# Two hybrid diffusion layers on one core: moving TensorE's streamed operands to other byte offsets

## What is computed

```python
for l in range(2):
    m  = split(silu(c) @ w_ada[l] + b_ada[l], 9)          # shift, scale, gate per part
    h  = h + 0.5 * m[2] * swiglu(modulate(rmsnorm(h)), w_in, w_out)      # 1024 -> 2*2816 -> 1024
    z  = modulate(rmsnorm(h)); p = z @ w_in_mix                          # 1024 -> 2048
    y  = concat(rg_lru_scans(p) * gelu(p), spatial_gate(p))
    h  = h + m[5] * (y @ w_out_mix)                                      # 1024 -> 1024
    h  = h + 0.5 * m[8] * swiglu(modulate(rmsnorm(h)), w_in, w_out)
return rmsnorm(h)
```

## Time and profile before

| | |
|---|---|
| two runs | 1577.13 and 1584.26 us, median 1580.7 us |
| span of the profiled execution | 1575.5 us |
| what lies around the span in the two runs | 1.6 and 8.8 us (5.2 at the median) |
| TensorE busy | 1561.2 us (99%), 9052 matmuls |
| weight loads busy | 1338.1 us (85%) |
| VectorE, ScalarE, GpSimd busy | 1001.6, 631.0, 82.5 us |
| from memory | 247.62 MB, 158 GB/s over the span |

### The profile page before, as it was taken

One profiled execution on the slowest core, in us unless ns is written; L12 is line 12 of the kernel. 1 busy time (PEld: TensorE's weight loads), 2 busy tenths in 40 slices (PEclk: granted clock), 3 DMA queues, 4 the chain that ended last, 5 costly groups with the idle time before them and its releaser, 6 DMA issues.

```text
span 1575.5 us, 22302 instructions
## 1 busy us (share of the span) xinstructions
PE 1561.2 (99%) x9052; PEld 1338.1 (85%) x9052; DVE 1001.6 (64%) x1243; ACT 631.0 (40%) x856; POOL 82.5 (5%) x100
## 2 busy tenths in 40 slices
PE   8999999999999999999999999999999999999998
PEld 6888888888988888888888898888888897999998
DVE  5776773783967577777364267777445358975554
ACT  4433322332784343323222243333232249764553
POOL 0000000011100200000000100000000111000001
PEclk9999999999999999999999999999999999999999
DMA  9565553653322355565353336556354323456563
GB/s 365 201 197 179 186 162 119 208 192 94 115 75 79 94 166 193 176 201 173 107 196 99 107 121 201 193 183 195 100 173 148 107 91 108 147 188 197 190 203 117
DMA packets 71786, 249.95 MB, mean 159 GB/s; under 512 B 11664, under 2 KB 11920, under 8 KB 70672
## 3 DMA queue, kind: packets, MB, share of 16 engines
q1 hardware_dynamic: 71696, 248.70, 48.1%
HBM read 247.62 MB, written 1.05 MB: 158 GB/s over the span
## 4 chain that ended last, share of the span: by engine, by line
PE 96%; DVE 2%; ACT 1%; issue 0%; POOL 0%; POOLq 0%; DVEq 0%; ACTq 0%
PE bank L437 85%; PE bank L574 2%; PE bank L580 2%; PE bank L576 2%; PE bank L452 1%; PE bank L475 1%; PE bank L747 1%; PE bank L720 1%; PE bank L718 1%; PE bank L719 1%; PE bank L749 0%; PE bank L468 0%; DVE w_lo L1174 0%; PE bank L529 0%; PE bank L460 0%
## 5 line engine op out<-in xcount | busy, mean ns | idle before, releaser
L877 ACT ACTIVATE w_hi<-raw 128x1024 fp32r<-128x1024 f32 x317 | 335.9, 1060 | 807.0 <-PE bank L437 792.8
L1174 DVE TENSOR_TENSOR w_lo<-raw,w_hi 128x1024 fp32r<-128x1024 f32 x317 | 387.7, 1225 | 371.9 <-ACT w_hi L877 371.6
L437 PE MATMUL bank<-z_hi,w_hi 128*128 128x512 f32 (+1 forms) x1480 | 535.9, 362 | 2.4 <-DVE w_lo L1174 1.9
L437 PE MATMUL bank<-z_lo,w_hi 128*128 128x512 f32 (+1 forms) x1480 | 532.1, 360 | 0.0
L437 PE MATMUL bank<-z_hi,w_lo 128*128 128x512 f32 (+1 forms) x1480 | 531.9, 359 | 0.0
L437 PEld LDWEIGHTS bank<-z_hi,w_hi 128*128 128x128 f32 x1480 | 278.0, 188 | 49.7 <-DVE w_lo L1174 3.2
L437 PEld LDWEIGHTS bank<-z_hi,w_lo 128*128 128x128 f32 x1480 | 278.0, 188 | 42.6
L437 PEld LDWEIGHTS bank<-z_lo,w_hi 128*128 128x128 f32 x1480 | 278.1, 188 | 42.6 <-issue 1.0
L437 PE MATMUL bank<-h_hi,w_hi 128*128 128x512 f32 (+1 forms) x770 | 266.5, 346 | 0.0
L437 PE MATMUL bank<-h_lo,w_hi 128*128 128x512 f32 (+1 forms) x770 | 265.7, 345 | 0.0
L437 PE MATMUL bank<-h_hi,w_lo 128*128 128x512 f32 (+1 forms) x770 | 265.6, 345 | 0.0
(11 more groups left out here) (185 smaller groups left out, 1234.3 us busy)
## 6 DMA issues: line engine op xcount, KB each, us to landing
raw<-weights SPq DMA_DIRECT2D x320, 512.0 KB, 4.1
ada_raw<-ada_w SPq DMA_DIRECT2D x128, 512.0 KB, 4.2
ada_head<-head_w SPq DMA_DIRECT2D x8, 1024.0 KB, 18.5
res<-x_t SPq DMA_DIRECT2D x4, 512.0 KB, 4.8
ada_raw<-gate_w SPq DMA_DIRECT2D x4, 256.0 KB, 5.3
ws<-sgu_w SPq DMA_DIRECT2D x2, 256.0 KB, 4.0
bs<-sgu_b SPq DMA_DIRECT2D x2, 256.0 KB, 4.2
out<-final SPq DMA_DIRECT2D x2, 256.0 KB, 3.0
```

What stands on the lines that cost most here:

```text
L437: m = pe.matmul(bank[:, to], w, x[:, k, at], start=start and i == 0, stop=stop and i == 2, skip_group_check=True)
L877: act.activation(w_hi[:, r, :], raw[:, r, :], ACT.Copy).then_inc(hi_ready, 1)
L1174: dve.tensor_tensor(w_lo[:, r, :], raw[:, r, :], w_hi[:, r, :].bitcast(F32), ALU.subtract).then_inc(lo_ready, 1)
```

## The change

Three unused tensors are added to the layout: 32 bytes ahead of `down_acc` and `z`, 96 bytes ahead of `raw`, and 96 bytes ahead of everything that shares the last space. Nothing else is changed: each engine has the same instructions in the same order, on other addresses. Lines of the kernel after are 1 to 3 higher (L437 is L440).

```diff
         res = sb("res", [P, KD, T])
 
+        sb("z_shift", [P, 8])
         with ExitStack() as down_scope:
             down_acc = [sb(f"down_acc{i}", [P, 2, D], F32, down_scope) for i in range(2)]
         with ExitStack() as end_scope:
             final = sb("final", [P, KD, SEQ], F32, end_scope)
         z_hi = sb("z_hi", [P, KD, T], F32R)
         z_lo = sb("z_lo", [P, KD, T], F32R)
+        sb("raw_shift", [P, 24])
         raw = sb("raw", [P, RING, SLOT])
...
         base_gain = sb("base_gain", [P, KD])
 
+        sb("h_shift", [P, 24])
         with ExitStack() as head_scope:
```

## The result

The changed kernel takes **1620.6 us** (median of two runs, 1620.42 and 1620.78) against 1580.7 before: 1.0251 of the time, with a 95% interval of 1.0209 to 1.0292. It is slower, and lies just above the range.

A forecast was written before the change was run, and what follows sets the result against it. TensorE's own pace was taken to bound the kernel (busy 1561.2 of 1575.5 us). The mean of three estimates (-41, -34, -15), -30 us, gave a span of 1545.5, plus 5.2 for the runs' median: 1551 us, range 1528 to 1620.

The forecast's parts named there:

- What a new offset is worth: TensorE matmuls: gain from distances of 32 or 96 bytes, drawn from the paces at 0 and 64; mean -30 us.
- three ways of going on: TensorE matmuls: left-over as a step (-41), a slope over offsets (-34), or by distance, 32 and 96 halfway (-15).
- The bounds of the pace: TensorE: below, streaming alone, 213.3 ns wide, 1502 us; above, 0.24 us per wide matmul, 1655 us.
- The slower rival: L437, TensorE: distances 32 or 96 never settle, wide 22 us more, ALONE 10.6 more; 1613 us (1600 to 1650), chance 0.29.
- disturbed pace: Where the gate matmuls disturb the even 226.7 ns, nine wide ones take 231.1 ns each; the slower rival's ground.
- The rival of no change: TensorE: left-over has another cause, or wide settles at 32 columns at any offset; 1581 us (1570 to 1590), chance 0.22.
- The 6198 matmuls: TensorE matmuls counted as moving against their weights from offset 0: 4938 wide and 1260 narrow.
- The rest of the change costs nothing: VectorE, ScalarE and DMA at offsets 32 and 96 cost nothing; `ada_head` landing 0 to 2 us, taken as 0.
- z and h would differ: Sign in the timeline's wide matmuls: if they differ, the slope is right, h near 217 ns, z near 223.
- The rule of the Trainium skill: TensorE has two independent SBUF read ports, weight loads take no bandwidth; an offset is worth nothing, the time stays.

The follow-up runs named there:

- The table: Short kernels without the computation: fp32r matmuls at 35 stream-to-weights distances, 512 and 256 columns wide; at distance 0, 226.7 and 120.0 ns between starts.
- the short kernels: Kernels of matmul stretches only, without the computation, varying distance, load width, start moment or type; wide fp32r at distance 0 with full loads: 226.7 ns.
- the kernel changed by 64: Against the kernel before, z and h both lie 64 bytes further from their weights, by three unused tensors: 1609.61 us, 1.0186 of before.

## Why the prediction was wrong

**The step that failed is "What a new offset is worth".** It took the 6.7 ns that 256-column matmuls have less at "64" for what 512-column ones would gain, and drew lines from there to 32 and 96. The table shows that a distance that is good for one width isn't so for the other, and that wide ones can only lose: 4938 of them sat on their best distance. All three ways of going on (-41, -34, -15 us) rested on it. Its second fault is the unit: within 128 bytes, the 192 of the `ALONE` columns looked like 64, and z's 160 like 32. The good distances of the two widths, 0 for 512 columns and 192 for 256, were taken as points on one line.

**The bounds of the pace.** 213.3 ns was a poor lower end; no wide fp32r stretch here came under 226.7. The upper one, 240 ns, held: the worst measured is 237.9.

**The slower rival** (0.29) was the right case: a distance of 32 or 96 off the weights doesn't reach the settled 226.7, and `ALONE` is taken off its good place. Its terms against what was measured: 22 us for wide ones, from 231.1 ns, where z takes 234.3 to 234.9, h and y 233.3 to 233.8, so some 24 + 10 + 0.7 = 35; 10.6 us for `ALONE`, where z lost 6.4 (984 x 6.5) and h 1.8, since 32 keeps half of the gain: 8. In sum 43 and not 33. The rows that I took for a disturbed pace were a passage of seven matmuls, of 228 to 236 ns, after which TensorE settled on 226.7 again. The timeline of the kernel before, just behind it:

```profile
421.75 0.39 PE L718 MATMUL bank<-w_hi,z_hi 128*128 128x512 f32 x1
...
422.43 0.39 PE L718 MATMUL bank<-w_hi,z_hi 128*128 128x512 f32 x1
```

Three matmuls in 0.68 us are 226.7 ns each. A wrong distance isn't a disturbance that goes on, but a pattern of its own, and a longer one. The rival also says "never settle", which is wrong in the words: it does settle, in the short kernels within some ten matmuls, and for good.

**The rival of no change** is refuted in both its grounds. The loops don't make 113.3 (in the kernel changed by 64 they run at 120), and only at distance 0 do wide matmuls with full loads settle on 32 columns over their stream, not at any distance. What spoke for it, `y_alone` at 117.7, was the second pace of distance 192.

**What held.** TensorE's pace goes through to the end one for one (42.6 of 43.1 us). The 6198 matmuls and the `ALONE` ones were the right ones to count. "The rest of the change costs nothing": means and landings are those of before, and `ada_head` at offset 96 lands in 18.4 us; z's first wide matmul behind those on the last piece of `ada_head` starts at 40.4 us instead of 39.7, within the 0 to 2 us I allowed. That z and h would differ, and that `ALONE` would show whether "64" was good of its own, were the right things to look at.

**The rule of the Trainium skill** that I set against the change, two independent read ports in "TensorE: Matmul & The Clock Gate", "Step-by-step: what each phase is for", makes an offset worth nothing. For bf16 at 512 columns this case agrees: 215.8 ns at eight distances. The same page of the Trainium skill, section "Back-to-back issue gap", gives 512/2.4 + 2.5 = 215.8 for the gap of an isolated matmul and some 131 ns for a stream of pairs of weight load and matmul; the bf16 matmuls here each have a load and take the first, not the second. For fp32r this case doesn't agree with the two ports: 226.7 to 237.9 ns with nothing changed but the distance. I was right to go against it and wrong on the sign.

## What to carry to other kernels

With fp32r matmuls back to back and a new weight load for each, choose where tensors lie by the distance from the start of the weights to the start of the stream, modulo 256 bytes: 0 for 512 columns, 192 (or 112, tried in one stretch only) for 256 columns. This holds for loads of 128 columns: with loads of 64, 160 was the best of six distances (226.7 ns, where 0 had 229.9). A tensor put anywhere in the layout, even one that nothing reads, moves all that lie behind it, and here three of them cost 2.5%; so pin these distances, and measure a few before a gain at one width is carried over to another.

## What the runs showed of the hardware

- For fp32r the pace of back-to-back matmuls depends on the distance of stream and weights modulo 256 bytes, at some distances on the moment of the start as well, and on nothing else of their place that was tried: 226.7 to 237.9 ns at 512 columns, 113.3 to 130.0 (at 104 bytes) at 256. For bf16 at 512 columns it doesn't.
- The patterns repeat: 226.67, 113.33 and 120.0 ns after each matmul, 466.7 after two (128 and 192 at 512 columns), 700 after three (96), 593.3 after five (128 and 160 at 256 columns), 1640 after seven (160). These are multiples of 6.67 ns, 16 cycles at the granted 2.4 GHz. Which part of TensorE has that step, and what in the load and the stream meets there, stays open; that it isn't the length of the load alone is shown.
- Distance 192 at 256 columns has two paces, 113.3 and 117.8 ns, and a stretch keeps the one it fell into. In the last part of the kernel before 1512 matmuls are at that distance: 1512 x 4.45 = 6.7 us. Its runs lie in two groups, near 1578 and near 1584 (1577.13 and 1584.26 in the first two). The kernel with everything moved together, which keeps the distances, has the same two groups: six of its ten runs at 1577.3 to 1579.3, four at 1583.8 to 1586.2. In the kernel with h alone moved, the profile caught one of the two longer executions, and z's loop had the slower pace in it, 4.3 us longer. I take this to be what sets the two groups apart; no longer execution of before was profiled, so it is not shown. The kernel after, with no narrow loop at 192, has both its runs within 0.4 us, which are too few to tell.
- A better layout wasn't found. The 1260 narrow matmuls at distance 0 (120.0 ns) share their tensors with the wide ones, for which 0 is the best. Of what lies by itself only `y_alone` (120 matmuls against the ring, 4.4 ns, 0.5 us) could gain over before, which is less than can be measured, and it wasn't tried.
